# A hybrid decoder step on one core: the mixer in another order, low weight parts on VectorE, nine expert matrices loaded early, experts in a ring of three

## What is computed

```python
xn = rms_norm(x);  h = xn @ w_in                     # 1024 -> 512 p, u, v, a, b and 3 x 1024 gates
ya = pool(p) @ pool_w * scale                         # trailing means over 2, 4, 8, 16 rows, less the row
yb = u * (tril(w_s) @ layer_norm(v) + b_s)            # SGU, per chunk of 128 rows and head
yc = silu(layer_norm(conv31(a * sigmoid(b))))         # causal depthwise convolution, 31 taps
merged = sig(gA) * (ya @ wA) + sig(gB) * (yb @ wB) + sig(gC) * (yc @ wC)
h = x + merged @ w_out
e0, e1 = two best experts of the best group of rms_norm(h)
y = h + sum of gate * ((silu(hn @ w_gate[e]) * (hn @ w_up[e])) @ w_down[e])
out = rms_norm(y)
```

## Time and profile before

| What | us |
|---|---|
| Median of the runs (1085.18 to 1085.79) | 1085.69 |
| Time of the profiled execution | 1083.14 |
| Its span, first to last instruction | 1081.2 |
| Start to the first weight product | 37.45 |
| Mixer, to the last product of w_out | 480.4 |
| Routing, to the first gate/up product | 41.7 |
| Experts, to the last down product | 486.9 |
| Last sums and norms | 34.7 |

### The profile page before, as it was taken

The page is one execution under the profiler, slowest core; times in us unless marked ns, Lnnn a source line. Parts: engine busy times, 40 slices in busy tenths (PEclk is TensorE's granted clock), DMA queues, the critical chain, the costliest instruction groups (busy, mean ns, idle before and its releaser), DMA issues.

```text
span 1081.2 us, 13667 instructions
## 1 busy us (share of the span) xinstructions
PE 857.3 (79%) x5197; PEld 585.3 (54%) x5197; DVE 383.5 (35%) x571; ACT 201.5 (19%) x304; POOL 313.7 (29%) x234
## 2 busy tenths in 40 slices
PE   1999978548999999899649888788788778778750
PEld 1999978438999999899323333232223223222210
DVE  4406999986468455421540000000000000000008
ACT  3323212023212343302500100000000000000003
POOL 2244999125334324321010211111101111111104
PEclk9999989759999999899859999999999999999995
DMA  7522220012222212262869899999999999999935
GB/s 218 145 78 88 68 77 22 20 32 96 78 78 78 98 59 78 83 234 78 319 254 403 344 420 420 419 420 421 419 420 419 421 420 420 420 422 419 421 142 212
DMA packets 73643, 261.74 MB, mean 242 GB/s; under 512 B 8999, under 2 KB 42947, under 8 KB 48480
## 3 DMA queue, kind: packets, MB, share of 16 engines
q1 hardware_dynamic: 68496, 252.44, 59.4%
q0 software_dynamic: 5120, 8.93, 2.2%
HBM read 256.08 MB, written 13.74 MB: 250 GB/s over the span
## 4 chain that ended last, share of the span: by engine, by line
PE 37%; DMA 25%; DVE 18%; issue 11%; POOL 4%; ACT 3%; SPq 1%; DVEq 0%; POOLq 0%; ACTq 0%
DMA gu<-in_w_up_e 24%; PE ps L815 14%; DVE work L1144 11%; PE ps L588 10%; PE ps L629 5%; POOL w_low L1450 4%; PE ps L836 4%; DVE xh L1104 1%; PE ps L562 1%; DVE xh L1419 1%; DMA xh<-in_x_prompt 1%; PE ps L804 1%; DVE xh L1411 1%; PE ps L673 1%; ACT w_high L886 1%
## 5 line engine op out<-in xcount | busy, mean ns | idle before, releaser
L1450 POOL TENSOR_TENSOR w_low<-ring,w_high 128x2048 fp32r<-128x2048 f32 (+1 forms) x38 | 155.6, 4097 | 237.1 <-ACT w_high L886 236.9
L588 PE MATMUL ps<-x_high,w_high 128*128 128x272 f32 x640 | 174.8, 291 | 7.2 <-POOL w_low L1450 7.2
L1373 DVE TENSOR_TENSOR work<-ps,norm_cols 128x512 f32<-128x512 f32 x32 | 22.1, 692 | 442.0 <-PE ps L804 442.0
L588 PE MATMUL ps<-x_low,w_high 128*128 128x272 f32 x640 | 173.4, 289 | 0.0
L1144 DVE SCALAR_TENSOR_TENSOR work<-slot,param,work 128x512 f32<-128x512 f32 x240 | 162.6, 755 | 1.2 <-DVE work L1201 1.2
L1531 POOL DMA_INDIRECT expert_rows<-xx,idx_now x32 | 32.9, 1027 | 387.9 <-ACT xx L1059 356.2
L815 PE MATMUL ps<-gu,work 128*64 128x512 f32 x512 | 118.4, 617 | 20.0 <-DMA gu<-in_w_up_e 17.4
L588 PE MATMUL ps<-x_high,w_low 128*128 128x272 f32 x640 | 133.1, 289 | 0.0
L815 PE MATMUL ps<-slot,work 128*64 128x512 f32 x480 | 111.2, 617 | 20.8 <-issue 20.0
L588 PEld LDWEIGHTS ps<-x_high,w_high 128*128 128x128 f32 x640 | 121.4, 190 | 8.5 <-issue 4.7
L588 PEld LDWEIGHTS ps<-x_low,w_high 128*128 128x128 f32 x640 | 121.1, 189 | 0.0
(11 more groups left out here) (239 smaller groups left out, 1065.9 us busy)
## 6 DMA issues: line engine op xcount, KB each, us to landing
ring<-in_w_down_e SPq DMA_DIRECT2D x16, 2048.0 KB, 22.2
gu<-in_w_gate_e SPq DMA_DIRECT2D x16, 2048.0 KB, 17.2
gu<-in_w_up_e SPq DMA_DIRECT2D x16, 2048.0 KB, 23.4
slot<-in_w_gate_e SPq DMA_DIRECT2D x15, 2048.0 KB, 17.3
slot<-in_w_up_e SPq DMA_DIRECT2D x15, 2048.0 KB, 23.4
slot<-in_w_down_e SPq DMA_DIRECT2D x15, 2048.0 KB, 22.2
ring<-in_w_in SPq DMA_DIRECT2D x22, 1024.0 KB, 5.1
ring<-in_w_out SPq DMA_DIRECT2D x4, 1024.0 KB, 7.8
```

The source lines that it names most:

```text
L588: last = pe.matmul(ps[:, 2 * r + half, 0:HT], w[:, k, c * P:(c + 1) * P], part[:, k, half * HT:(half + 1) * HT], start=(k == 0 and len(par ...
L1373: v.tensor_tensor(xgT[s].rearrange("p c (h t) -> p c h t", h=2), ps[:, s].rearrange("p (c h t) -> p c h t", c=4, h=2), wide(norm_cols[:].r ...
L1450: g.tensor_tensor(w_low[s][:, 0:kt], wring[s][:, 0:kt], w_high[s][:, 0:kt].bitcast(F32), ALU.subtract).then_inc(low_ready, 1)
```

## The change

The mixer gets another order. TensorE takes b, a, v, p, the SGU products, u, the states, the gates and products of branch A, then those of B, then the gates of C with the two channel sums of the convolution's norm between them, and the products of C. `place_next` deals the four result slots out in turn, and each slot has a semaphore of its own (`slot_free`). All 36 low parts from pair 2 on are made by VectorE (`low`), in an order written out with the taps in pieces between them (`taps`); the sample columns of the convolution come from one product with overlapping windows and one reduction (`conv_sample`); the pool branch moves to VectorE too (`pool_branch`). GpSimd makes the first two low parts and then has nothing to do in the mixer.

One area of memory holds the mixer's tensors and three full expert places. Six matrices of the nine are asked for inside and behind the w_out loads, three after the last product of w_out. Expert e goes to the place of expert e - 3. The rows are stored without their norm; its factor is carried through the tables (`rstd_of`) and applied behind the products, by ScalarE's scale and in VectorE's product. GpSimd takes the gather's index straight from the table. All engines have the 32 experts written out instead of loops.

```diff
@@ SyncE @@
+        sp.wait_ge(product, done("gC7"))
+        load_gate_up(0, 0)
+        load_pair(OUT)
+        load_gate_up(0, 1)
+        load_pair(OUT + 1)
+        load_down(0)
+        load_pair(OUT + 2)
...
+        load_pair(OUT + 3)
+        load_gate_up(1, 0)
+        sp.wait_ge(product, done("bC7"))
+        load_gate_up(1, 1)
         sp.wait_ge(low_ready, len(pairs))
-        load_down(0, 0)
-        sp.wait_ge(product, N_O)
-        load_gate_up(0, 0, 0)
-        load_gate_up(0, 0, 1)
-        load_gate_up(1, 1, 1)
-        load_down(1, 1)
...
+        load_down(2)
...
+        sp.wait_ge(product, rows_done(1, NCH - 1))
+        load_gate_up(2, 0)
+        load_down(1)
+        load_gate_up(2, 1)
...
+        for e in range(3, NE):
+            sp.wait_ge(gu_done, e - 2)
             for m in range(2):
-                load_gate_up(e, s, m)
-            sp.wait_ge(dn_done, after)
-            load_down(e, s)
...
+                load_gate_up(e, m)
+            sp.wait_ge(dn_done, e - 2)
+            load_down(e)
@@ TensorE, experts @@
-        with pe.Fori(0, NE // 2 - 2) as i:
-            for w in range(2):
-                e = 2 * i + 3 + w
-                gate_up(e, 1 - w, w, i + 2, e - 1)
...
+        for e in range(NE):
+            gate_up(e, e % 2, e % 3, e // 3 + 1)
+            if e + 1 < NE:
+                turn_rows(e + 1, (e + 1) % 2, (e + 1) // 2)
+            turn_hidden(e, e % 2)
+            down(e, e % 2, e % 3, e // 3 + 1)
@@ VectorE @@
+        def low(n):
+            s, kt = n % 2, row_tiles(n)
+            dve.wait_ge(high_ready, n)
+            v.tensor_tensor(w_low[s][:, 0:kt], wring[s][:, 0:kt], w_high[s][:, 0:kt].bitcast(F32), ALU.subtract).then_inc(low_ready, 1)
...
+            own(v.tensor_tensor(prod, ahead, wide(w.unsqueeze(1).unsqueeze(1), [P, NSEQ, STEP, TAPS]), ALU.mult))
+            own(v.tensor_reduce(yc[:, q, SEQ:T], products.rearrange("p (n k) -> p n k", k=TAPS), AX, ALU.add))
...
-            tap(k, k if k else None)
...
+        for j in range(NJ):
+            low(20 + 2 * j)
+            taps(3)
+            low(21 + 2 * j)
+            merge("B", j)
+            taps(8 if j < NJ - 1 else KW * TAPS - n_taps[0])
...
+            v.scalar_tensor_tensor(hid[s], ps[:, 2 + s, 256:512], rstd_of[:, bass.ds(e, 1)], sig[s],
@@ GpSimd @@
-        def low_part(s, n, kt=KD):
...
-            g.tensor_tensor(w_low[s][:, 0:kt], wring[s][:, 0:kt], w_high[s][:, 0:kt].bitcast(F32), ALU.subtract).then_inc(low_ready, 1)
```

More of the change, by code:

```diff
@@ L110, in next_place @@
         return (nc.sbuf_base + 31) // 32 * 32
-    def over(name, shape, dt, tensor_at, first=0):
-        return nc.alloc_sbuf_tensor_at(name, shape, dt, offset=tensor_at + 4 * first)
     def sem(name):
         return ctx.enter_context(nc.semaphore(name))
[L119 to L131, removed]
+    ctx.enter_context(nc.allow_non_contiguous_dma(reason="transposed SGU weights"))
+    M = 4 * D
+    AREA = 9 * M + 7424
+    area_at = next_place()
+    area = sb("area", [P, AREA])
+    xg_rows = sb("xrows", [P, NCH * D])
     cst = sb("cst", [P, NCONST])
@@ L150, in program @@
[L150 to L161, removed]
-    y_low = [over(f"y_low{b}", [P, KW, T], F32R, ybr_at, b * KW * T) for b in range(3)]
@@ new lines, in program, with row_tiles, place, place_next @@
+    OUT = len(pairs)
+    pairs += [d["w_out"][0][:, j * 256:(j + 1) * 256] for j in range(4)]
+    def row_tiles(n):
+        return pairs[n].shape[0] // P
+    placed = {}
+    frees = [0] * 4
+    def place(names, slots):
+        need = tuple(frees)
+        for name, r in zip(names, slots):
+            frees[r] += 1
+            placed[name] = (r, len(placed) + 1, need[r], frees[r])
+    turn_at = [0]
+    def place_next(*names):
+        for name in names:
+            place([name], [turn_at[0] % 4])
+            turn_at[0] += 1
@@ L638, in _ @@
[L638 to L659 removed]
+            last.then_inc(product, 1)
@@ new lines, in _ @@
+        take_p(1)
+        high(8)
+        take_p(2)
+        take_p(3)
+        high(9)
+        for q in range(KW):
+            act.wait_ge(*taken(f"p{q}"))
+            last = s_.copy(pool_steps(pext[:, q])[:, :, PH:], pext[:, q, PRAW:PRAW + NS].rearrange("p (b i) -> p b i", i=STEP))
+        last.then_inc(p_steps_in, 1)
+        act.wait_ge(product, done("u1"))
+        high(10)
+        for h in range(2):
+            act.wait_ge(*taken(f"u{h}"))
+            s_.copy(y_high[1][:, h], yb[:, h]).then_inc(sgu_high, 1)
@@ new lines, in _ @@
+        act.wait_ge(product, done("u3"))
+        high(11)
+        for h in range(2, KW):
+            act.wait_ge(*taken(f"u{h}"))
+            s_.copy(y_high[1][:, h], yb[:, h]).then_inc(sgu_high, 1)
+        for i, rows in enumerate((PH, CH)):
+            act.wait_ge(product, done(f"state{i}"))
+            r = placed[f"state{i}"][0]
+            s_.copy(states[0:rows, 2 * i], ps[0:rows, 2 * r]).then_inc(states_in, 1)
+            s_.copy(states[0:NS, 2 * i + 1], ps[0:NS, 2 * r + 1]).then_inc(slot_free[r], 1)
@@ L1220, in _ @@
+        low(GC + 3)
+        dve.wait_ge(product, done("var"))
+        v.tensor_scalar(halves(row_a[:]), of("var"), 1.0 / W, EPS, ALU.mult, ALU.add).then_inc(freed("var"), 1)
         dve.wait_ge(root, 3)
```

1427 lines of the change are left out of this document (719 added, 708 removed).

## The result

The changed kernel takes 1028.76 us (median of 4 runs, 1027.61 to 1030.01) against 1085.43 for the kernel before; the ratio over the runs is 0.9484, 95% interval 0.9462 to 0.9507 (that of the two medians is 0.9478). Forecast were 1030 and a range of 1014 to 1054. The profiled execution spans 1025.8 us against 1081.2.

The account below looks back on a forecast made before the run. TensorE bounds the mixer, small steps the routing, weight DMA the experts: mixer to 473, first gate/up at 516.3, stream from 527 for 454.5 to 981.7, then 10, 34.7, 1.9 and 2.5: 1030 us, range 1014 to 1054.

Parts of the forecast that it names:

- TensorE's own work: Mixer: TensorE's products stay the same in number and shape and take 423.4 us in all.
- the hole: Mixer, 184 to 233.6: TensorE's 32.6 us of idle time behind the block of convolution taps should close.
- the loose products: Mixer: pool maps, state turns and sample steps on TensorE, estimated at 8.4 us.
- the two large kinds: Mixer: 2496 products of 272 columns and 720 of 256 columns, 315.6 + 85.7 us.
- Its waits: Mixer: TensorE still waits for v, the convolution's norm and ahead of w_out, 12 us in sum, bounds 0 and 36.
- The low parts: Mixer: 36 of 38 go from GpSimd to VectorE, 70 us more there, with room in total.
- rival (1): Mixer: VectorE's order makes low parts late, 2 us at each of twelve pairs, 24 us, giving 1054; chance 0.16.
- Routing: From last residual sum to first gate/up product: 41.1 us as before, plus 1.5, bounds -1 and +3.
- The stream: Experts: weights begin at 527, 190.9 MB at 420 GB/s without a gap, 454.5 us, to 981.7.
- rival (2): Experts: the weight stream has gaps at its start as before, 8 to 18 us, giving 1038 to 1048; chance 0.09.
- Rival (4): Experts: written-out code must be fetched while DMA is full, making it slower than before, possibly above 1190; chance 0.05.
- Rival (3): Experts: the weight stream runs slower, at 381 GB/s, taking 501 us and giving 1077; chance 0.02.

Follow-up runs that it names:

- low_gpsimd: The changed kernel with all 38 low parts back on GpSimd, the taps still strewn: 1031.16 us, +2.4 to the changed kernel.
- half_down: The changed kernel, loading only the upper half of each down matrix from expert 3 on: 987.40 us, -41.4 to the changed kernel.
- warm: The changed kernel with 102 extra products, results unread, in TensorE's three waits of the routing: 1085.36 us, +56.6 to the changed kernel.
- ask_later: The changed kernel with every reload of an expert's place asked for one expert later, nine matrices still early: 1043.29 us, +14.5.
- five_edits: The changed kernel with branch C's last merge and m's low parts earlier, 25 extra routing products, expert 3's gate/up halved, sample sums on VectorE, early square root: 1015.13 us.

## Why the prediction was right, and where it was not

*TensorE's own work and the hole.* 420.5 us against 423.4; the loose products took some 3.5 us and not the 8.4 that I had estimated, and the two large kinds together 2 more than their terms. The hole closed as forecast. Its waits were 9.2 us against 12: 1.5 for v (3), 7.1 for w_out (7.5 + 0.6), none for the convolution's norm (1), and 0.6 for branch A's low part, which I had not listed. The mixer ended at 466.9, not 473. Taps took 0.74 us and a low part 2.29, as the rows of before had told; a group of sample columns took 3.2 us and not 2.5, and VectorE in all 251 us and not 290.

*The low parts.* I gave them 70 us on VectorE and room for them, which held, and rival (1) did not happen: between the pairs one weight load waits 1.0 us for a low part, and no product does. (Ahead of w_out a low part is one link of the 7.1 us, as forecast.) What the prediction did not say is that the move is worth next to nothing by itself. low_gpsimd shows it. With the taps back in a block nothing of the 51 us is left; how much of them the rest of the new order is worth by itself stays open.

*Routing.* 43.2 us from the last product against 0.7 + 41.1 + 1.5. Right.

*The stream.* This is the term that was mis-sized. I had it start at 527, flat at 420 GB/s, and end square: 454.5 us to 981.7, and the last product 10 us behind it. It was asked for at 519.27, its last bytes came near 983, and the last product ended 7.3 later. The window of the whole stream:

```profile
520.00:983.00 463.00, 382.79 (x1664) 140.67 (x1666) 33.61 (x62) 45.02 (x94) 61.31 (x60) 0.96 1.00 414
```

That is 191.7 MB, not 190.9 (2 us); 0.7 us passed ahead of the first byte, and the first 20 us ran below the rate (1.4); and at the end the share of busy DMA engines fell in steps, 374 GB/s from 970 to 976 (share 0.90) and 159 to 983 (0.39): these 3.36 MB would have taken 8 us at 420 and took 13 (5). Start 7.7 earlier, stream 9.2 longer, last step 2.7 shorter: 990.3 against 991.7. The median also lay 1.15 us above the profiled execution, where I had added 2.5. So 1030 for 1028.76 is better than the steps deserve: the misses had opposite signs. A hint stood in the earlier trace rows, where 1035 to 1040 still moves 79 GB/s; I read the stream as ended there.

The rate itself was right, 417 to 420 GB/s. The Trainium skill, "HBM Reference", section "Specifications (TRN2)", tells a core that streams alone (about 425 GB/s) from two that share (358 each); with the first this trace agrees, and it is the sentence that belongs to this kernel, not the one that the prediction weighed.

*The third place and the early matrices.* From 530 to 970 there is no gap, so rival (2) did not happen; undoing the one part costs 14.5, by the start alone, the other 8 us. That the experts as a whole are only 6.7 us shorter than before has its cause in the start. There the stream was asked for 0.4 us after the first product began (559.98, 559.60) and had moved its bytes by 1040, 480 us. Here all places are full, and it is asked for when the first product has ended, 9.2 us after its beginning, and takes 463.7: 16.3 less (10 for two matrices fewer, some 5 for the gaps of the earlier trace rows), less 8.8 for the later start, less 0.8 at the last product. I had the 9 us in my sum and had not seen that they take back half of what the places bring.

*Code.* Rival (4) is out: 13.34 us an expert against 13.28, and in half_down, where no weights are waited for, the gate/up products have no wait without a releaser left. The page counts 42 packets of instruction fetch on the larger queue, 17 before.

*Rate.* Rival (3) is out by the window from 620 to 960.

## What to carry over

Where an engine works in order, a long block of work that nobody needs yet costs what stands behind it, so place it in pieces between the steps that others wait for; which engine does the small steps mattered far less here, as long as no such block stood beside them. A stream that runs at its full rate makes what delays its first request count nearly one for one (59.4 us at the last product for 59.3 at the request in warm, 18.1 for 18.3 in ask_later, 8.7 for 10.4 in five_edits), so that request is the place to look for time. Its end is not square: count some us for the share of DMA engines that falls off (5 here). And before an instruction is used as filler, take its price from a row of the very shape, and count how many instructions make one product.

## What had not been expected of the hardware

A GpSimd instruction of 4.57 us took 76.71 beside 120 VectorE instructions of two SBUF inputs back to back, which lost nothing (0.66 us each with it and without). The instructions of a product of 512 columns with 128 columns of weights came 0.43 us apart, two to a product; those with 64 columns of weights, writing in turn to two halves of the partitions, came 0.215 apart at the same clock. And TensorE, busy for most of a stretch, was granted less than its full clock in parts of it (0.69 in 5.4 us of half_down, 0.81 for the first product of five_edits); keeping it busy ahead of a product did not reliably give the upper level, 7.11 us in one kernel (warm, with extra products nearly without a break ahead of it) and 8.81 in another (five_edits, with waits between them).
